# Turning softmax weights by VectorE's 32x32 transposes and DRAM trips instead of TensorE transposes, in a decoder layer

## The reference

```python
h = rmsnorm(x, mix_norm_pre)
dq, dk, dv, sq, sk, sv, gates = split(h @ w_in)        # 2048 columns in, 8704 out
# 8 "diff" heads: two score maps each, head size 64, values 128 wide, causal, ALiBi
p = softmax(scores + bias)                             # (2 maps, 256 queries, 256 keys)
a = p[0] - lam * p[1]
ya = (rmsnorm(a @ v, subln) * 0.2) @ w_branch_diff
# 16 "window" heads: window 128, one sink logit a head, 4 shared key/value heads, head size 64
p = softmax(concat(scores + bias, sink))[..., :-1]
yb = (p @ v) @ w_branch_swa
y = (sigmoid(ga) * ya + sigmoid(gb) * yb) @ w_out
x = x + rmsnorm(y, mix_norm_post)
```

## Time and profile before

| what | value |
|---|---|
| median of 3 runs | 2000.96 us (2000.74 to 2001.69) |
| span of the profiled execution | 1999.0 us |
| TensorE busy | 1975.9 us, 99% of the span |
| VectorE busy | 1474.4 us, 74% |
| ScalarE busy | 1069.8 us, 54% |
| GpSimd busy | 113.4 us, 6% |
| TensorE's mean granted clock | 0.998 |

### The profile page before, as it was taken

One profiled execution on the slowest core, in us unless ns is written; L12 is line 12 of the kernel. 1 busy time (PEld: TensorE's weight loads), 2 busy tenths in 40 slices (PEclk: granted clock), 3 DMA queues, 4 the chain that ended last, 5 costly groups with the idle time before them and its releaser, 6 DMA issues.

```text
span 1999.0 us, 23190 instructions
## 1 busy us (share of the span) xinstructions
PE 1975.9 (99%) x9010; PEld 1639.6 (82%) x9010; DVE 1474.4 (74%) x1710; ACT 1069.8 (54%) x1384; POOL 113.4 (6%) x194
## 2 busy tenths in 40 slices
PE   8999999999999999999999999999999999999997
PEld 6888888889888878888888888888888888988886
DVE  6888888767877765556655675688888887678676
ACT  6555555545555554445555554465555654555453
POOL 0000000000000001110100010000000001000000
PEclk9999999999999999999999999999999999999999
DMA  6777777857566757864444577567786777666563
GB/s 235 240 237 235 238 239 234 260 185 241 201 210 215 250 188 235 246 209 153 158 158 148 168 245 229 189 211 232 230 254 222 236 246 248 195 226 220 180 242 137
DMA packets 207374, 431.06 MB, mean 216 GB/s; under 512 B 10225, under 2 KB 18722, under 8 KB 206114
## 3 DMA queue, kind: packets, MB, share of 16 engines
q1 hardware_dynamic: 195794, 388.16, 58.9%
q0 software_dynamic: 11008, 38.28, 6.6%
q10 hardware_dynamic: 464, 3.15, 0.4%
HBM read 409.37 MB, written 20.19 MB: 215 GB/s over the span
## 4 chain that ended last, share of the span: by engine, by line
PE 94%; DVE 3%; ACT 2%; issue 1%; DMA 0%; POOL 0%; DVEq 0%; POOLq 0%; ACTq 0%
PE acc L761 17%; PE acc L763 17%; PE acc L762 17%; PE acc L688 9%; PE acc L690 9%; PE acc L689 9%; PE tp L763 4%; PE tp L761 4%; PE tp L762 4%; PE tp L974 1%; PE tp L948 1%; PE tp L715 1%; ACT junk L1143 1%; ACT w_hi L1064 1%; PE tp L958 1%
## 5 line engine op out<-in xcount | busy, mean ns | idle before, releaser
L1085 ACT ACTIVATE w_hi<-raw 128x1024 fp32r<-128x1024 f32 (+1 forms) x400 | 404.1, 1023 | 314.7 <-PE acc L763 212.3
L1458 DVE TENSOR_TENSOR w_lo<-raw,w_hi 128x1024 fp32r<-128x1024 f32 (+1 forms) x400 | 464.9, 1177 | 137.5 <-ACT w_hi L1085 135.0
L1425 DVE TENSOR_TENSOR w_lo<-raw,w_hi 128x1024 fp32r<-128x1024 f32 x215 | 260.5, 1222 | 212.8 <-ACT w_hi L1064 212.6
L761 PE MATMUL acc<-w_hi,h_hi 128*128 128x512 f32 (+1 forms) x928 | 354.3, 382 | 0.7 <-DVE w_lo L1458 0.7
L763 PE MATMUL acc<-w_hi,h_lo 128*128 128x512 f32 (+1 forms) x928 | 354.1, 382 | 0.0
L762 PE MATMUL acc<-w_lo,h_hi 128*128 128x512 f32 (+1 forms) x928 | 354.0, 382 | 0.0
L1064 ACT ACTIVATE w_hi<-raw 128x1024 fp32r<-128x1024 f32 x215 | 224.5, 1055 | 192.7 <-PE acc L690 191.3
L1109 ACT ACTIVATE w_hi<-raw 128x1024 fp32r<-128x1024 f32 (+1 forms) x217 | 214.0, 996 | 196.4 <-PE acc L763 125.5
L1696 DVE TENSOR_TENSOR w_lo<-raw,w_hi 128x1024 fp32r<-128x1024 f32 (+1 forms) x217 | 244.6, 1143 | 89.8 <-ACT w_hi L1109 87.5
L688 PE MATMUL acc<-w_hi,h_hi 128*128 128x512 f32 x736 | 292.7, 398 | 5.3 <-DVE w_lo L1425 5.1
L690 PE MATMUL acc<-w_hi,h_lo 128*128 128x512 f32 x736 | 287.8, 391 | 0.0
(11 more groups left out here) (212 smaller groups left out, 2374.5 us busy)
## 6 DMA issues: line engine op xcount, KB each, us to landing
raw<-in_ffn_w_in SPq DMA_DIRECT2D x126, 1024.0 KB, 5.1
raw<-in_w_in SPq DMA_DIRECT2D x68, 1024.0 KB, 5.3
raw<-in_ffn_w_out SPq DMA_DIRECT2D x56, 1024.0 KB, 5.1
raw<-in_ffn_w_in SPq DMA_DIRECT2D x68, 512.0 KB, 4.5
raw<-in_ffn_w_out SPq DMA_DIRECT2D x48, 512.0 KB, 4.9
raw<-in_w_out SPq DMA_DIRECT2D x16, 1024.0 KB, 5.1
bounce<-blocks POOLq DMA_DIRECT2D x29, 512.0 KB, 3.7
blocks<-bounce POOLq DMA_DIRECT2D x116, 128.0 KB, 4.3
```

The lines of the kernel that those rows point to most:

```text
L761: nc.tensor.matmul(o[:, 0:width], x[0], wh, start=first, stop=False)
L1085: nc.scalar.activation(w_hi[:, s % 4, 0:n], raw[:, g % 4, s % 2 * 2:s % 2 * 2 + n], ACT.Copy)\
L1425: nc.vector.tensor_tensor(lo, raw[:, g % 4, s % 2 * 2:s % 2 * 2 + 2], hi.bitcast(F32), ALU.subtract).then_inc(lo_ready, 1)
L1458: nc.vector.tensor_tensor(w_lo[:, s % 4, 0:n], raw[:, g % 4, s % 2 * 2:s % 2 * 2 + n], w_hi[:, s % 4, 0:n].bitcast(F32), ALU.subtract).the ...
```

## The change

The softmax weights of a unit no longer go through TensorE and PSUM. Behind `mix(u)`, VectorE transposes the 32x32 blocks of `sc` into `p_blocks`. GpSimd writes `p_blocks` to DRAM and reads it back into `pt` with four transfers. `pt` now holds the three blocks (and the two heads) of one query next to each other, so that a block is read with a step of 3 floats in head units and 6 in window units. `pv(u)` moves from 4u+6 to 4u+8, where it stands behind `scores(u+2)`; `take_o`, the squares, the variance and the scaling move to 4u+9, 4u+12, 4u+13 and 4u+17. The trip of unit u+2 stands ahead of the root of head u on GpSimd; those of the last units stand behind the last root. TensorE's transposes and ScalarE's copies fall away.

```diff
-        pt = sb("pt", [P, 2, 2, 3 * P], F32, at + 4 * 76 * SEQ)
+        pt = sb("pt", [P, 2, 2 * 3 * P], F32, at + 4 * 76 * SEQ)
+        p_blocks = sb("p_blocks", [P, 2 * 3 * P], F32, at + 4 * 82 * SEQ)
...
+        p_bounce = [nc.dram_tensor(f"p_bounce{n}", (P, n * 3 * P), F32, kind="Internal").ap() for n in (1, 2)]
...
+            def move_p(u):
+
+                n = 1 if u < HEADS else 2
+                held, x = p_bounce[n - 1], n * 3 * P // 4
+                gp.wait_ge(p_turned, u + 1)
+                if u:
+                    gp.wait_ge(p_in, 64 * u)
+                gp.dma_start(held, p_blocks[:, 0:4 * x]).then_inc(p_out, 16)
+                gp.wait_ge(p_out, 16 * (u + 1))
+                if u >= 2:
+                    gp.wait_ge(pv_done, u - 1)
+                rows_of = held.rearrange("(q c) (b x) -> b c q x", q=4, b=4)
+                for b in range(4):
+                    dst = pt[32 * b:32 * b + 32, u % 2, 0:4 * x].rearrange("c (q x) -> c q x", q=4)
+                    gp.dma_start(dst, rows_of[b]).then_inc(p_in, 16)
...
             for i, (n, m) in enumerate(ROOT_STEPS):
+                if R_HEAD <= n < R_HEAD + HEADS:
+                    u = n - R_HEAD
+                    for v in range(0 if u == 0 else u + 2, u + 3):
+                        move_p(v)
                 gp.wait_ge(var_ready, i + 1)
...
                 elif n == R_HEAD + HEADS - 1:
+                    for u in range(HEADS + 2, UNITS):
+                        move_p(u)
                     for i in range(Z_TRIPS):
...
-            def turn_p(u):
-                pe.wait_ge(mixed, u + 1)
-                if u:
-                    pe.wait_ge(o_read, u)
-                for c in range(1 if u < HEADS else 2):
-                    for b in range(3):
-                        mm = nc.tensor.transpose(tp[:, c, b * P:(b + 1) * P], sc[:, u % 2, c, b * P:(b + 1) * P],
-                                                 ident[:])
-                mm.then_inc(p_turned, 1)
-
             def pv(u):
-                pe.wait_ge(p_copied, u + 1)
+                pe.wait_ge(p_in, 64 * (u + 1))
+                if u:
+                    pe.wait_ge(o_read, u)
...
-                for c in range(1 if u < HEADS else 2):
+                heads = 1 if u < HEADS else 2
+                turned_p = pt[:, u % 2, 0:heads * 3 * P].rearrange("p (n e j) -> p e j n", e=heads, j=3)
+                for c in range(heads):
...
-                            mm = nc.tensor.matmul(o, pt[:, u % 2, c, b * P:(b + 1) * P], v,
+                            mm = nc.tensor.matmul(o, turned_p[:, c, b], v,
...
-                hooks.setdefault(4 * u + 4, []).append(lambda u=u: turn_p(u))
-                hooks.setdefault(4 * u + 6, []).append(lambda u=u: pv(u))
+                hooks.setdefault(4 * u + 8, []).append(lambda u=u: pv(u))
...
-                nc.scalar.activation(pt[:, u % 2, 0:n], tp[:, 0:n, 0:3 * P], ACT.Copy).then_inc(p_copied, 1)
...
+            def turn_p(u):
+
+                heads = 1 if u < HEADS else 2
+                dve.wait_ge(mixed, u + 1)
+                if u:
+                    dve.wait_ge(p_out, 16 * u)
+                turned_p = p_blocks[:, 0:heads * 3 * P].rearrange("p (b c e j) -> p e b j c", b=4, e=heads, j=3)
+                for c in range(heads):
+                    ins = nc.vector.transpose(turned_p[:, c],
+                                              sc[:, u % 2, c, :].rearrange("p (j b c) -> p b j c", b=4, j=3))
+                ins.then_inc(p_turned, 1)
...
-                hooks.setdefault(4 * u + 3, []).append(lambda u=u: mix(u))
-                hooks.setdefault(4 * u + 7, []).append(lambda u=u: take_o(u))
+                hooks.setdefault(4 * u + 3, []).append(lambda u=u: (mix(u), turn_p(u)))
+            for u in range(UNITS):
+                hooks.setdefault(4 * u + 9, []).append(lambda u=u: take_o(u))
                 if u < HEADS:
-                    hooks.setdefault(4 * u + 10, []).append(lambda u=u: head_var(u))
-                    hooks.setdefault(4 * u + 12, []).append(lambda u=u: head_scale(u))
+                    hooks.setdefault(4 * u + 13, []).append(lambda u=u: head_var(u))
+                    hooks.setdefault(4 * u + 17, []).append(lambda u=u: head_scale(u))
```

More of the change, by code:

```diff
@@ L287, in layer_kernel @@
         sc = sb("sc", [P, 2, 2, 3 * P], F32, at + 4 * 70 * SEQ)
-        pt = sb("pt", [P, 2, 2, 3 * P], F32, at + 4 * 76 * SEQ)
-        assert 82 * SEQ <= 2 * FT * SEQ
+        pt = sb("pt", [P, 2, 2 * 3 * P], F32, at + 4 * 76 * SEQ)
+        p_blocks = sb("p_blocks", [P, 2 * 3 * P], F32, at + 4 * 82 * SEQ)
+        assert 85 * SEQ <= 2 * FT * SEQ
         spare = 4 * (FAST_PAIRS[-1]) * SEQ
@@ L399, in layer_kernel @@
         p_turned = sem("p_turned")
-        p_copied = sem("p_copied")
+        p_out = sem("p_out")
+        p_in = sem("p_in")
         pv_done = sem("pv_done")
@@ L950, in scores, with pv @@
                 mm.then_inc(scored, 1)
-            def turn_p(u):
-                pe.wait_ge(mixed, u + 1)
+            def pv(u):
+                pe.wait_ge(p_in, 64 * (u + 1))
                 if u:
                     pe.wait_ge(o_read, u)
-                for c in range(1 if u < HEADS else 2):
-                    for b in range(3):
-                        mm = nc.tensor.transpose(tp[:, c, b * P:(b + 1) * P], sc[:, u % 2, c, b * P:(b + 1) * P],
-                                                 ident[:])
-                mm.then_inc(p_turned, 1)
-            def pv(u):
-                pe.wait_ge(p_copied, u + 1)
                 if u == 0:
                     pe.wait_ge(acc_free[1], 2 * (U_C + 4))
-                for c in range(1 if u < HEADS else 2):
+                heads = 1 if u < HEADS else 2
+                turned_p = pt[:, u % 2, 0:heads * 3 * P].rearrange("p (n e j) -> p e j n", e=heads, j=3)
+                for c in range(heads):
                     n = P if u < HEADS else HD
@@ L990, in turn_sk @@
                     turn(lambda t: stage[:, m, t * P:(t + 1) * P], 2 + m, 4)
-            hooks[4 * SK_UNIT + 2].insert(0, turn_sk)
+            hooks.setdefault(4 * SK_UNIT + 2, []).insert(0, turn_sk)
             def o_tile(k, m):
@@ L1334, in _ @@
                 hooks.setdefault(4 * u + 1, []).append(lambda u=u: exps(u))
-                hooks.setdefault(4 * u + 5, []).append(lambda u=u: copy_p(u))
                 if u < HEADS:
-                    hooks.setdefault(4 * u + 9, []).append(lambda u=u: square_o(u))
+                    hooks.setdefault(4 * u + 12, []).append(lambda u=u: square_o(u))
             def o_hi(q):
@@ L1916, in mix @@
                 dve.wait_ge(exp_ready, u + 1)
+                if u >= 2:
+                    dve.wait_ge(o_read, u - 1)
                 if u < HEADS:
```

## The result

The changed kernel takes 2009.39 us (median of 4 runs, 2008.87 to 2010.23) against 2000.85 us (2000.73 to 2001.69): a ratio of 1.0042, with a 95% interval of 1.0031 to 1.0054. It is slower by 8.5 us where 7.2 us less had been forecast.

A forecast was written before the change was run, and what follows sets the result against it. TensorE's queue, busy 99% of the span, was taken as the bound. Removed transposes gave 7.2 us, all else 0: 1999.0 - 7.2 = 1991.8, plus 2.0 around the span, 1993.8 us; range 1990.8 to 2009.5.

The forecast's parts named there:

- Changed: the step at which TensorE reads the turned weights: Value products' loads at steps of 3 and 6 floats: taken as 0, bounds 0 to 15.7 us, called the weakest term.
- the 75 ns at which the prediction said it would fail: Sign of failure: the step costing over 75 ns more on each of 96 window loads, which cancels the 7.2 us.
- Transposes removed: 72 transposes leave TensorE's queue between scores and weight products: 7.2 us freed, or 10.2 at most.
- The 0.20 us for leaving the scores: Excess in the first weight product after scores, seen in unit 0 without transposes; expected to stay at 0.20 us.
- The trip: Turned weights through DRAM on GpSimd's queue: 11 us (bounds 10.1 to 15.3) in 14.0 or 15.4 us of room, cost 0.
- VectorE's transposes: One or two 128x384 block transposes a unit behind the mix: 0.53 us to twice that each, hidden.
- The first (slow strided loads, both kinds: 2009.5): Rival: value products' loads halved in pace, 10.3 us (window units) or 15.7 (both); chance 0.28, of which both 0.12.
- The second (late trip): Rival: turned weights land late for value products, 1.3 us a head unit, 10 us for eight, 2004 us; chance 0.16.
- the third (nothing freed): Rival: leaving the scores or waiting for two semaphores takes the transposes' time, staying near 2001 us; chance 0.08.

The follow-up runs named there:

- before_strided: Kernel before, with turned weights laid out and read in steps of 3 and 6 floats, transposes still on TensorE, no trip: 2013.02 us, ratio 1.0061.
- apart: Changed kernel with value products and outputs one hook later, away from the scores, last unit's unmoved, strided loads kept: 2003.43 us, ratio 1.0014.
- near_reads: Changed kernel with value products reading 128 neighbouring floats, in a wrong order, trip kept: 1991.12 us, ratio 0.9952.
- steps: Changed kernel with load steps of 1 to 5 floats, varied by unit, weights in a wrong order: 2000.02 us in one run.
- runs_out: Changed kernel with weights written to DRAM in four transfers of 128-byte runs, so neighbouring floats are read in the right order: 2003.81 us, ratio 1.0014.

## Why the prediction was wrong, point by point

**The step that failed** is "Changed: the step at which TensorE reads the turned weights", taken at zero. It measured 12.3 us (before_strided, by its pieces and by its total; apart against near_reads), inside its own bounds of 0 to 15.7: the window loads cost 9.8 of the 10.3 us at the upper end, the head loads 2.5 of 5.4. A window load costs 102 ns more ((2.51 - 1.28) / 12), above the 75 ns at which the prediction said it would fail. The argument for zero was that a load has a spare side, as its record runs beside the product ahead of it. But the record is 192 ns long against a pace of 107, so loads already overlapped by nearly half. The pace being the same for 64 and 128 columns should have been read the other way: what paces the window units is the load, and whatever lengthens it is paid. The runs show it: at a step of 3 floats a load takes 163 ns in head units (0.98 us for six) and 165 in window units (1.98 for twelve), whether 128 or 64 columns follow. The rule of the Trainium skill that spoke against the change (the same page and section as under steps) was weighed there, and set aside for an argument that no row carried.

**A term that was missing** is the clock. The sum held none, and no rival did; slow loads placed right behind scores cost 6.0 us beyond their own 12.3 (apart), some 5 of it the clock. Both parts are needed: before_strided has the loads without the place and near_reads the place without the loads, and neither shows a fall. Why this pair lets the clock fall, and behind three only of the six window units that stand behind scores, stays open.

**Transposes removed: right.** 7.2 us was the sum. From the first scores to the first turned output TensorE takes 1108.45 - 881.24 = 227.2 us before and 1100.42 - 881.09 = 219.3 us in near_reads: 7.9 us less. The 0.20 us for leaving the scores did stay, as 1.48 against 1.28 us in the list of steps shows.

**The trip: right in the main.** It was put at 11 us in a room of 14.0 and 15.4 (with the DMA share called half that of the stage before, where 0.5 against 0.79 is nearer to two thirds). In the chain, unit by unit, one head unit's goes: out, three of the issues, the last landing.

```profile
946.18 3.80 DMA p_bounce<-p_blocks
949.98 0.29 issue
950.27 1.63 POOL pt L652 x3
951.90 4.42 DMA pt<-p_bounce
```

That is 10.1 us. Unit 8's trip took 12.9 us, from its issue at 998.74 to 1011.6, and is the one for which TensorE waited. How little room was left is seen in runs_out, where longer trips were late three times. **VectorE's transposes: right.** They lay between the bounds of 0.53 us and twice that. They were hidden too: in the attention stage TensorE waited for no remainder.

```profile
L1951 DVE STREAM_TRANSPOSE p_blocks<-sc x24: 695/882/951, 893.6 to 1101.5; 128x384 f32<-128x384 f32 x24
```

In runs_out, where they write runs of 32 neighbouring floats, they took less:

```profile
L1952 DVE STREAM_TRANSPOSE p_blocks<-sc x24: 535/578/579, 892.9 to 1097.9; 128x384 f32<-128x384 f32 x24
```

**The rivals.** The first (slow strided loads, both kinds: 2009.5) named the cause, and its time is nearly the measured 2009.4 us, but partly by offset: its price was 3.4 us too high, the place behind scores took 6.0 us more, and near_reads is 2.7 us lower than the forecast. The second (late trip) did not happen here but for the 0.2 us of unit 8, nor did the third (nothing freed). The sum as measured: 1991.1 + 12.3 + 6.0 = 2009.4 us. It closes by construction, since near_reads, apart and the changed kernel give its terms; the 12.3 alone has a second source, before_strided.

Of the 2.7 us, 0.7 lie in the attention stage (7.9 against 7.2). The other two lie behind the last instruction that the timeline lists: from the end of SyncE's last transfers out to the end of the span there are 5.6 us in the kernel before and in before_strided, and 3.5 to 3.8 us in the changed kernel and in all six runs with the trip. The cause stays open. The last lines of before (span 1999.0 us) and near_reads (1988.8 us):

```profile
1991.07 2.32 SPq L579 DMA_DIRECT2D out<-xs  x4
...
1983.01 2.32 SPq L582 DMA_DIRECT2D out<-xs  x4
```

## What to carry to other kernels

A layout that saves an instruction may be paid for by whoever reads it: where TensorE is the bound and loads set the pace, as here, 128x128 float32 weights want neighbouring floats, or a step of two at most, so let the transfer put them in order. A chain full of DMA proves nothing until the list of waits says that the bound engine stood; and a trip that just fits wants a second buffer at its far end before anything is added to it.

## What the runs showed of the hardware that was not expected

- The pace of a 128x128 float32 load depends on the step in floats: 107 ns at 1, 114 at 2, 165 to 170 at 3, 216 to 228 at 4 and 5, 209 at 6 (2.51 us for twelve). Slow loads set the pace alike with 128 columns a product: 163 ns at a step of 3 (0.98 us for six against 0.67).
- TensorE's clock fell to its lower level with no idle time in front: behind scores that use 64 of the rows, followed at once by loads with a step of 5 or 6, in three of the six window units that stand behind scores, and in one of the two units of steps with a step of 5. It held with steps of 4 or less, and with a step of 6 away from scores. In runs_out it fell behind idle time.
- VectorE's 128x384 transposes took 0.70 to 0.95 us when they wrote with a step of 3 or 6 floats, and 0.54 to 0.58 us in runs_out, where they write runs of 32 neighbouring floats.
